# Two-layer hybrid attention and MoE trunk: expert rows gathered from the residual, one gate block of the first pair in the freed memory

## The reference, cut to what matters

```python
h = x                                             # (256, 1024)
for l in range(2):
    xn = rms_norm(h, ln_mix[l])
    h = h + (diff_sparse_mixer if l == 0 else chunk_band_mixer)(xn, ...)
    xn = rms_norm(h, ln_ffn[l])
    h = h + hier_moe(xn, ...)
return rms_norm(h, ln_final)

def rms_norm(x, g):
    return x * rsqrt(mean(x * x, -1) + 1e-6) * g

def hier_moe(xn, ...):                            # 32 experts, 2 chosen for each token
    combine = ...                                 # (256, 32), two non-zero entries in a row
    for e in range(32):
        h = silu(xn @ w_gate[e]) * (xn @ w_up[e])     # 1024 -> 512
        y = y + combine[:, e:e+1] * (h @ w_down[e])   # 512 -> 1024
```

## Time and profile before

| | |
|---|---|
| median of 3 runs | 1192.37 us (1189.73 to 1194.67) |
| the profiled execution | 1190.6 us, span 1188.8 us |
| granted TensorE clock | 0.996 of full speed |
| TensorE busy | 1122.9 us (94%) |
| VectorE, ScalarE, GpSimd busy | 217.4, 242.4, 116.0 us |
| data read | 441.5 MB, mean 372 GB/s over the span |
| chain that ended last | PE 64%, DMA 31%, DVE 3% |

### The profile page before, as it was taken

The page is one execution under the profiler, slowest core; times in us unless marked ns, Lnnn a source line. Parts: engine busy times, 40 slices in busy tenths (PEclk is TensorE's granted clock), DMA queues, the critical chain, the costliest instruction groups (busy, mean ns, idle before and its releaser), DMA issues.

```text
span 1188.8 us, 14009 instructions
## 1 busy us (share of the span) xinstructions
PE 1122.9 (94%) x5006; PEld 503.4 (42%) x5006; DVE 217.4 (18%) x579; ACT 242.4 (20%) x564; POOL 116.0 (10%) x307
## 2 busy tenths in 40 slices
PE   8999999999999888889999999999999998888897
PEld 6776543333333333333387756333333333333232
DVE  2864332000000000000223234400000000000002
ACT  2144241111211111111112233311121111111111
POOL 0002111000110000000000000200011000000001
PEclk9999999999999999999999999999999999999999
DMA  6984589999999999999998354899999999999994
GB/s 239 339 356 187 203 337 429 429 427 427 427 428 428 428 429 428 428 426 428 422 353 325 107 213 173 343 425 429 425 428 428 427 428 428 428 429 427 427 429 194
DMA packets 49163, 443.28 MB, mean 373 GB/s; under 512 B 9629, under 2 KB 14809, under 8 KB 17369
## 3 DMA queue, kind: packets, MB, share of 16 engines
q1 hardware_dynamic: 48040, 441.34, 89.5%
q10 hardware_dynamic: 1072, 1.26, 0.3%
HBM read 441.49 MB, written 1.09 MB: 372 GB/s over the span
## 4 chain that ended last, share of the span: by engine, by line
PE 64%; DMA 31%; DVE 3%; issue 1%; ACT 1%; SPq 0%; POOL 0%; ACTq 0%; POOLq 0%; DVEq 0%
PE PS L1535 23%; DMA places<-in_moe_w_up 12%; PE PS L1544 12%; DMA places<-in_moe_w_gate 11%; PE PS L1287 7%; DMA places<-in_moe_w_down 6%; PE PS L1551 6%; PE PS L1419 5%; PE PS L1291 4%; PE PS L1299 1%; PE PS L1374 1%; DMA bias<-in_c_rel_bias 1%; PE PS L1403 1%; PE PS L1504 1%; PE PS L1620 1%
## 5 line engine op out<-in xcount | busy, mean ns | idle before, releaser
L1535 PE MATMUL PS<-places,mix 128*64 128x512 f32 x1984 | 443.4, 596 | 45.6 <-DMA places<-in_moe_w_up 30.0
L1535 PEld LDWEIGHTS PS<-places,mix 128*64 128x64 f32 x1984 | 142.5, 137 | 337.9 <-issue 283.7
L1544 PE MATMUL PS<-places,gain_att 128*64 128x512 f32 x960 | 213.8, 596 | 0.8 <-ACT gain_att L806 0.5
L1551 PE MATMUL PS<-mix 128*128 128x512 f32 x256 | 124.8, 608 | 0.0
L759 ACT ACTIVATE mix<-acts 128x512 f32 x120 | 76.3, 636 | 226.1 <-PE PS L1535 213.8
L1544 PEld LDWEIGHTS PS<-places,gain_att 128*64 128x64 f32 x960 | 65.9, 137 | 124.4 <-issue 122.7
L1287 PE MATMUL PS<-acts,places 128*128 128x256 f32 x448 | 103.2, 384 | 0.0
L1186 DVE TENSOR_TENSOR mix<-PS,mix 128x512 f32<-128x512 f32 x28 | 19.4, 692 | 418.2 <-PE PS L1535 418.2
L1287 PEld LDWEIGHTS PS<-acts,places 128*128 128x128 f32 x448 | 83.2, 190 | 14.9 <-issue 3.7
L528 POOL TENSOR_TENSOR sm<-sm 128x1 f32<-128x1 f32 x32 | 6.2, 193 | 692.0 <-PE PS L1626 660.0
L567 POOL TENSOR_SCALAR mix<-drop 128x64 f32<-128x64 f32 x128 | 72.0, 579 | 0.0
(11 more groups left out here) (221 smaller groups left out, 629.5 us busy)
## 6 DMA issues: line engine op xcount, KB each, us to landing
places<-in_moe_w_gate SPq DMA_DIRECT2D x56, 2048.0 KB, 25.2
places<-in_moe_w_down SPq DMA_DIRECT2D x54, 2048.0 KB, 32.6
places<-in_moe_w_up SPq DMA_DIRECT2D x52, 2048.0 KB, 30.4
places<-in_moe_w_gate SPq DMA_DIRECT2D x16, 1024.0 KB, 10.8
places<-in_moe_w_up SPq DMA_DIRECT2D x16, 1024.0 KB, 6.0
places<-in_moe_w_down SPq DMA_DIRECT2D x16, 1024.0 KB, 7.5
places<-in_c_w_in SPq DMA_DIRECT2D x12, 1024.0 KB, 20.7
places<-in_ab_w_in SPq DMA_DIRECT2D x8, 1024.0 KB, 13.5
```

The costliest lines, as they stand in the source:

```text
L1535: last = mm(PS[e * SLOTS:(e + 1) * SLOTS, 2 + part, :], xg[:, k, e * SLOTS:(e + 1) * SLOTS], w[e][:, kk, :], start=(k == 0), stop=(k == NK ...
L1544: last = mm(PS[e * SLOTS:(e + 1) * SLOTS, 6 + b, :], hidT[:, k, e * SLOTS:(e + 1) * SLOTS], w[e][:, 512 * b:512 * b + 512], start=(k == 0) ...
L1551: last = mm(PS[:, Y_BANK[q]], pickT[:, t], ye[:, 512 * b:512 * b + 512], start=first, stop=final)
```

## The change

Four things change in each layer.

- `gather` multiplies by `h[:, t]` itself. `picks` puts rstd in place of the ones: two VectorE operations of the kind (equal, then times rstd) and one sum, in place of one comparison and one comparison with sum. ScalarE's two normed copies go, and with them TensorE's wait for `s_xn`.
- The memory of `xn` (`acts[:, 0:2048]`, one block) is free from the end of the mixer until `sorted_x[1]` is written. Block (0, 3), the last gate block of pair 0, goes there. In layer 0 its load waits until TensorE has turned the heads (`s_turn` 4), in layer 1 until the projection's input is scaled (`s_xs` 4).
- Place 3 is then free for block (1, 7), `FIRST_AHEAD`. It is loaded where (0, 3) was, and left out of the later loads.
- VectorE's first `gathered_copy` waits until four expert blocks are used, since it overwrites block (0, 3).

```diff
+BESIDE = (0, UP_CHUNKS - 1)
 def once(i, c):
+    if (i, c) == BESIDE:
+        return ONCE
     return c - OUT_CHUNKS if i == KEPT and 0 <= c - OUT_CHUNKS < ONCE else None
+FIRST_AHEAD = next(c for c in range(CHUNKS) if place_of(1, c) == place_of(*BESIDE))
...
+        pick_early = at(3264, SEQ)
...
             n = once(i, c)
             if n is None:
                 return place(place_of(i, c))
+            if n == ONCE:
+                return acts[:, 0:SLOT_W]
...
                 for c in range(CHUNKS):
                     if c < IN_CHUNKS[l]:
                         sp.wait_ge(s_proj[l], c + 1)
-                    chunk(l, 0, 0, c)
+                    if (0, c) == BESIDE:
+                        chunk(l, 1, 1, FIRST_AHEAD)
+                    else:
+                        chunk(l, 0, 0, c)
...
                 for c in range(OUT_CHUNKS + 1, OUT_CHUNKS + 1 + IN_BIAS):
                     chunk(l, KEPT, KEPT, c)
+                if l:
+                    sp.wait_ge(s_xs, 4)
+                else:
+                    sp.wait_ge(s_turn, 4)
+                chunk(l, 0, *BESIDE)
                 for m in range(OUT_CHUNKS):
                     sp.wait_ge(s_od[l], 3 + m + 1)
                     chunk(l, 1, 1, m)
...
                 for c in range(OUT_CHUNKS, CHUNKS):
+                    if c == FIRST_AHEAD:
+                        continue
                     sp.wait_ge(s_used[l], used_before(1, c))
                     chunk(l, 1, 1, c)
...
-                    act.wait_ge(s_rs, 2 * (2 * l + 1) + t + 1)
-                    act.activation(xn[:, t], h[:, t], ACT.Copy, scale=rstd[:, t:t + 1]).then_inc(s_xn, 1)
...
-                link(dve.tensor_scalar(pick[:, t], iota, late[:, t:t + 1], None, ALU.is_equal))
-                dve.scalar_tensor_tensor(pick[:, t], iota, early[:, t:t + 1], pick[:, t], ALU.is_equal, ALU.add).then_inc(s_pk, 1)
+                dve.tensor_scalar(pick[:, t], iota, late[:, t:t + 1], rstd[:, t:t + 1], ALU.is_equal, ALU.mult)
+                link(dve.tensor_scalar(pick_early, iota, early[:, t:t + 1], rstd[:, t:t + 1], ALU.is_equal, ALU.mult))
+                dve.tensor_tensor(pick[:, t], pick_early, pick[:, t], ALU.add).then_inc(s_pk, 1)
...
                 dve.wait_ge(s_xg[l], 3 * b + 4)
+                if b == 0:
+                    dve.wait_ge(s_used[l], BESIDE[1] + 1)
...
                 pe.wait_ge(s_pk, NT * l + t + 1)
-                pe.wait_ge(s_xn, NT * l + t + 1)
...
-                        last = mm(PS[:, bank, kk * SEQ:(kk + 1) * SEQ], xn[:, t, k * P:(k + 1) * P], pick[:, t], start=True, stop=True)
+                        last = mm(PS[:, bank, kk * SEQ:(kk + 1) * SEQ], h[:, t, k * P:(k + 1) * P], pick[:, t], start=True, stop=True)
```

More of the change, by code:

```diff
@@ L355, in build @@
         s_place = [[sem(f"loaded{l}_{p}") for p in range(PLACES)] for l in range(DEPTH)]
-        s_once = [sem(f"once_{n}") for n in range(ONCE)]
+        s_once = [sem(f"once_{n}") for n in range(ONCE + 1)]
         s_proj, s_pa, s_pd = per_layer("projected"), per_layer("proj_act"), per_layer("proj_dve")
@@ L509, in _ @@
                             two_chunks(l, (g * ROUND + i) % PAIRS, i, c)
-            for q, signal, count in ((0, s_xn, DEPTH * NT + 1), (1, s_xua, NK // 2 + 1), (3, s_xn, DEPTH * NT + 2)):
+            for q, signal, count in ((0, s_xn, 1), (1, s_xua, NK // 2 + 1), (3, s_xn, 2)):
                 t, cols = q // 2, slice(q % 2 * D // 2, (q % 2 + 1) * D // 2)
```

## The result

| | before | after |
|---|---|---|
| median of 20 runs each | 1192.36 us | 1193.61 us |
| profiled execution | 1190.6 us, span 1188.8 | span 1190.9 |

The ratio to before is 1.0016, 95% interval 1.0008 to 1.0023: slower by 1.9 us (the two medians alone lie 1.25 us apart). The prediction was 1188.0 us, within 1184.8 to 1191.8. It missed the range and the sign.

What follows compares the result with a forecast made beforehand. The DMA load queue was taken to end each layer, so a block carried in its valley gains up to 2.45 us: 1.9 in layer 0 plus 2.45 in layer 1, 1192.37 - 4.35 = 1188.0 us, range 1184.8 to 1191.8.

Steps and rivals of the forecast that it cites:

- the delay ends in VectorE's own wait for the logits: Tile 0's pick matrix before gather: its longer computation, about 0.3 us, was to be absorbed there.
- The pick: Pick matrix on VectorE before gather: 0.3 us longer, delaying TensorE's expert work, felt only at the gates.
- the copies of tile 1: VectorE's four gathered copies: start about 166.9, end near 169.9, hidden before the product with 3.6 us to spare.
- The block: Block (1, 7) loaded in the valley: worth 1.9 us in layer 0 and 2.45 in layer 1, 4.35 in all.
- 4.9 + 2.45 = 7.35: Assumed time from issue to landing of a 2 MB double load into an empty queue; 8.45 us from above.
- first gate: Double load waiting for ten used blocks: issued at 179.4 in layer 0; room for 1.9 us there, 2.6 in layer 1.
- 3 x 2.45 = 7.35: Time for three single blocks behind (1, 8), ending at 181.0 in place of 183.6 in layer 0.
- The second gate: Later double load, waiting until pair 3 is used: room for 3.0 us in layer 0, 3.5 in layer 1.
- 6.8 us: Estimate for one double load from the skill's rule of about 2.0 us plus bytes over 436,000.
- the difference between the layers: Called chance: 16 KB instruction blocks on the same DMA engines can make the last landing late.
- the one that ended slower, at 1193.5: Rival, chance 0.06: gathered copies come too late, delaying VectorE's product and TensorE by up to 2.8 us per layer.
- the one in which the gates take most of the gain: Rival, chance 0.22: slower landings at the gates or badly placed instruction blocks leave about 2 us gain, 1190.4 us.

Runs made afterwards that it cites:

- e3: Changed kernel without the block moved ahead (loads and gathered copies as before); 1194.60 us, ratio 1.0024 to the kernel before.
- e2: Changed kernel with the old pick matrix, so only the block moved ahead; 1191.81 us, ratio 0.9996 to the kernel before.
- e5: Kernel before with ten small matmuls per layer between pair 0's up and down blocks, ahead of the first gate; 1196.84 us, ratio 1.0031.
- e6: Kernel before with ten small matmuls per layer ahead of pair 2, between the two gates; 1194.82 us, ratio 1.0018.
- e7: e3 plus three small matmuls per layer in TensorE's waits before gather; 1192.71 us, ratio 0.9997 to the kernel before.
- e10: Kernel before plus three small matmuls per layer in TensorE's waits before gather, nothing else; 1191.93 us, ratio 0.9996.
- e1: Changed kernel plus three small matmuls per layer in TensorE's waits before gather; 1191.56 us, ratio 0.9994 to the kernel before.
- e4: e1 with the first double load, (2, 0) with (2, 1), split into two single loads; 1190.75 us, ratio 0.9990 to the kernel before.
- e8: e4 with the pick's operation for late issued ahead of the subtraction giving early; 1190.17 us, ratio 0.9974 to the kernel before.
- e11: e8 run again unchanged, on another chip; 1190.20 us, ratio 0.9984 to the kernel before.
- e12: e8 with the last gain's load moved from layer 1's fourth pair to behind ScalarE's loop over the pairs; 1189.50 us, ratio 0.9977.

## Why the prediction was wrong

**The clock: a missing term, 2.6 us.** The prediction said of tile 0 that "the delay ends in VectorE's own wait for the logits", and looked only at who waits for whom: this step failed, since it put the cost of TensorE's new wait at nothing. TensorE before went from the router logits, which end at 147.6 to 147.7, into gather at 147.61 with no wait. The 0.33 us that pick got longer opened a wait of 0.23 us, on top of one of 0.39 us for ScalarE that ended 1.1 us earlier, and the clock fell to one half for 3.4 us, in layer 0 from about 148.2, in layer 1 from about 738.7. In the eight profiles of kernels with work in these waits the clock fell at none of 16 gathers; without it at all four with the longer pick (after, e3), and at four of eight with the old one (before, e2, e5, e6). e3 against e7 gives its price: two gathers that take 1.6 us longer each, block (1, 4) issued 1.3 us later each, 2.6 us in the two layers and 3.2 by the ratios. As before pays 1.0 us for a fall in some executions, the change's own share is smaller than that; how much smaller is open.

**The pick: right in size, 0.33 for 0.3,** and in place for tile 1: block (1, 4) comes 0.33 us later in each profile without a fall. In the time it can't be told from nothing (e7 against e10, 0.9997 and 0.9996).

**The normed copy and the copies of tile 1: right.** Nothing came sooner for the two activations saved. The copies run at 168.81, later than the 166.9 foreseen by the delay, and end 4.3 us ahead of the product. Timeline of VectorE, after:

```profile
168.81 2.48 DVE L1129 TENSOR_TENSOR acts<-PS,br_gain 128x512 f32<-128x512 f32 x4 [8.93 <-PE PS L1554]
175.58 0.76 DVE L1204 TENSOR_TENSOR mix<-PS,mix 128x256 f32<-128x256 f32 x2 [4.29 <-PE PS L1554]
```

**The block: mechanism right, size wrong.** It was to bring 4.35 us. By the ratios it brings 0.3 (e1 against e7), 0.5 (e2) or 1.0 (after against e3), each uncertain by over 1 us; by the traces 1.3. The failed step is "I take the 1 MB time and one more block, 4.9 + 2.45 = 7.35". At the first gate a double load takes 9.0 to 10.0 us from issue to landing in after, e1 and e2, in both layers; before it took 9.6 and 10.2. On average that is 0.4 us less, where the prediction had room for 1.9 and 2.6.

Two parts of the sum were too short. The queue was not nearly empty at the issue: the three blocks behind (1, 8) end 7.6 to 9.3 us after it, not 3 x 2.45 = 7.35, and the last of them lands 2.3 to 3.6 us after the double load's issue, where the sums had 1.6 and 1.5. And the double load lands 6.3 to 7.0 us behind that block in five of six cases (5.4 in layer 1 of e2), against 4.7 to 5.6 in the kernels without the block. There the gate holds the queue. With the two single loads of e4, e8 and e11 it is 5.2 to 5.8. The second gate, said to have 3 us of room, takes 9.0 to 9.4 in layer 0 (before 10.6), and 10.5 to 11.3 in layer 1 (before 11.2), most likely with the gain's load in it.

Where a gate binds, the queue follows the issue by TensorE: a microsecond lost ahead of the gate moves the end of the layer, while the missing block only makes the queue wait. e5 and e6 show this in the kernel before for the greater part, not in full: 3.7 and 2.1 us of the 4.9 and 5.2 held in the two layers.

By the rule of the Trainium skill, "DMA: Bandwidth & Descriptors", section "Anatomy of one DMA", the prediction estimated 6.8 us, further off than its own floor; measured are 9.0 to 10.0. The section fits that rule to DMAs issued by GpSimd, and the prediction left that out: the loads here are issued by SyncE.

Why the load takes so long is only partly shown. A load of 1 MB at the same place takes 8.1 (e4), and the prediction added to the shortest landings in an empty queue, when the rows had 5.6 and 6.0 too. Blocks of instructions fall in this stretch, one near 182 us before and one near 184 after, which may hold up one DMA engine each time. No run takes them away, so the prediction's word that they make the difference between the layers is not shown either.

**The sum.** Without the clock's fall the change stands at 0.9994 (e1), with it at 1.0016. In the two profiles the spans give the result: 3.3 us lost up to block (1, 4) in the two layers (0.33 and 1.3 us in each), 1.7 gained behind it, so 1.6 of the 2.1 us between the spans of 1188.8 and 1190.9. Another 0.44 was there before the first changed wait, at 139.06. Of the rivals none was the case: the one that ended slower, at 1193.5, came within 0.1 us of the median by luck, since its mechanism, the late copies, didn't occur; and the one in which the gates take most of the gain was right in its half and had no clock in it. The text's own tests did work: the time to landing above 8.5 us and the matmuls more than 0.5 us late were named as what would prove it wrong.

## What to carry to other kernels

A wait of 0.2 to 0.3 us ahead of a product can cost more than itself, here 1.3 us at a time, when the clock falls behind it: look at the granted clock and at the waits just before, not only at whether the new wait is short, and put small matmuls into them before anything else is judged. To price a block moved ahead, take the time to landing at the gate from the same place in the program, not the best landing elsewhere, and test the room with a hold in the old kernel, its length read from the trace, before building the new one. When runs differ by less than their noise, compare spans between two fixed instructions in the traces: they told 0.33 us from nothing here. Two halves of a change that are hidden by one another (here a clock that cost about 2.6 us, a block whose gain was small) only come apart when each is run alone.

## What the runs showed of the hardware that was not expected

- The granted clock fell from 1.00 to 0.50 at gather behind two waits of 0.39 and 0.23 us within 1.7 us of a TensorE that otherwise worked (after and e3, both layers), and in some executions behind the first of them alone, with the old pick (e2, e5, e6). In after it stayed low for 3.4 us.
- On VectorE an operation of equal, then times a scalar from memory took 0.41 us for 128 x 256 (after), the one without the factor 0.35 (before); the sum of two such tensors 0.43. Two that don't wait for one another start 0.33 us apart (147.12 and 147.45).
- With a load of 0.5 MB on another queue, issued 0.07 us after a double load, this landed about 1 us later (e11 9.9, e12 without it 8.9 us), one profile each.
